# Where GpSimd issues the accumulating transfers of the first product's weight sums: behind the first mixer and about the norm, instead of inside the mixer

## The reference

```
# first block
h = rms_norm(x, ln_pre_mix);  proj = h @ w_in          # pooled features, q, k, v of 12 heads
mix = concat(multi_scale_pool(...), dilated_attention(rope(q), rope(k), v)) @ w_out
x = x + rms_norm(mix, ln_post_mix)
h = rms_norm(x, ln_pre_ffn)
f = (silu(h @ w_gate) * (h @ w_up)) @ w_down           # inner width 2816
x = x + rms_norm(f, ln_post_ffn)
# second block: three kinds of attention, then h + conv_gated_mlp(...) with w_up_2 and w_down_2,
# then a gated per-layer embedding with w_ple_gate_2 and w_ple_proj_2
```

## Time and profile before

| what | before |
| --- | --- |
| median of 3 runs | 1268.55 us (1266.91 to 1269.29) |
| profiled execution, its time | 1270.42 us |
| profiled execution, its span | 1268.7 us |
| TensorE busy | 1254.4 us, 99% of the span |
| GpSimd busy | 512.3 us, 40% |
| VectorE busy, ScalarE busy | 949.8 us, 729.0 us |
| mean granted clock of TensorE | 0.998 |

### The profile page before, as it was taken

The page is one execution under the profiler, slowest core; times in us unless marked ns, Lnnn a source line. Parts: engine busy times, 40 slices in busy tenths (PEclk is TensorE's granted clock), DMA queues, the critical chain, the costliest instruction groups (busy, mean ns, idle before and its releaser), DMA issues.

```text
span 1268.7 us, 22131 instructions
## 1 busy us (share of the span) xinstructions
PE 1254.4 (99%) x7684; PEld 1142.8 (90%) x7684; DVE 949.8 (75%) x1732; ACT 729.0 (57%) x1437; POOL 512.3 (40%) x578
## 2 busy tenths in 40 slices
PE   8999999999999999999999999999999999999998
PEld 7999978989999988889999999889889999887887
DVE  6687765799988878884566778457987777789754
ACT  5666744545555556656667778435455555556452
POOL 5576781256655500126788866310121313000000
PEclk9999999999999999999999999999999999999999
DMA  7699732335444467522377953232323333565221
GB/s 232 223 202 235 170 92 100 99 132 202 165 132 165 142 239 217 141 76 76 67 159 139 166 105 89 95 103 90 100 83 93 103 98 99 197 242 166 68 99 67
DMA packets 145607, 173.45 MB, mean 137 GB/s; under 512 B 25420, under 2 KB 111643, under 8 KB 145522
## 3 DMA queue, kind: packets, MB, share of 16 engines
q1 hardware_dynamic: 129600, 145.15, 35.8%
q0 software_dynamic: 15920, 27.18, 12.1%
q10 hardware_dynamic: 2, 0.00, 0.0%
HBM read 170.22 MB, written 39.85 MB: 166 GB/s over the span
## 4 chain that ended last, share of the span: by engine, by line
PE 88%; DVE 6%; POOL 2%; ACT 1%; DMA 1%; issue 1%; ACTq 0%; DVEq 0%; POOLq 0%
PE ps L2844 13%; PE ps L2845 13%; PE ps L2846 13%; PE ps L2963 6%; PE ps L2970 6%; PE ps L2965 6%; PE ps L3096 3%; PE ps L3100 3%; PE ps L3098 3%; PE ps L3140 3%; PE ps L3142 3%; PE ps L3141 3%; PE ps L3058 2%; DVE w_lo L2393 2%; PE ps L3046 1%; PE ps L3047 1%
## 5 line engine op out<-in xcount | busy, mean ns | idle before, releaser
L2844 PE MATMUL ps<-h_hi,w_hi 128*128 128x256 f32 (+1 forms) x748 | 238.3, 319 | 0.0
L2845 PE MATMUL ps<-h_lo,w_hi 128*128 128x256 f32 (+1 forms) x748 | 237.4, 317 | 0.0
L2846 PE MATMUL ps<-h_hi,w_lo 128*128 128x256 f32 (+1 forms) x748 | 237.2, 317 | 0.0
L2963 PE MATMUL ps<-w_hi,h_hi 128*128 128x384 f32 (+2 forms) x512 | 162.6, 328 | 0.0
L2965 PE MATMUL ps<-w_hi,h_lo 128*128 128x384 f32 (+2 forms) x512 | 157.9, 319 | 0.0
L2846 PEld LDWEIGHTS ps<-h_hi,w_lo 128*128 128x128 f32 x748 | 142.6, 191 | 9.6
L2844 PEld LDWEIGHTS ps<-h_hi,w_hi 128*128 128x128 f32 x748 | 142.6, 191 | 9.1 <-DVE h_lo L2140 0.3
L2845 PEld LDWEIGHTS ps<-h_lo,w_hi 128*128 128x128 f32 x748 | 142.7, 191 | 8.5
L1281 POOL TENSOR_TENSOR w_lo<-w_raw,w_hi 128x384 fp32r<-128x384 f32 (+2 forms) x114 | 120.5, 1131 | 26.9 <-ACT w_hi L1524 26.7
L2970 PE MATMUL ps<-w_lo,h_hi 128*128 128x384 f32 (+2 forms) x512 | 101.5, 319 | 0.0
L3140 PE MATMUL ps<-w_hi,st_hi 128*128 128x512 f32 x252 | 98.6, 391 | 0.5 <-DVE st_lo L2404 0.2
(11 more groups left out here) (327 smaller groups left out, 3338.9 us busy)
## 6 DMA issues: line engine op xcount, KB each, us to landing
w_raw<-in_w_up_dram SPq DMA_DIRECT2D x25, 1024.0 KB, 5.3
w_raw<-in_w_in_dram SPq DMA_DIRECT2D x69, 256.0 KB, 4.1
w_raw<-in_w_gate_dram SPq DMA_DIRECT2D x11, 1024.0 KB, 5.3
down_sums<-in_w_down_dram SPq DMA_DIRECT2D x18, 512.0 KB, 5.9
down_sums<-in_w_down_dram SPq DMA_DIRECT2D x36, 256.0 KB, 6.0
down_sums<-in_w_down_dram POOLq DMA_DIRECT2D x12, 768.0 KB, 8.3
down_sums<-down_sums POOLq DMA_DIRECT2D x12, 768.0 KB, 8.7
w_raw<-in_w_out_dram SPq DMA_DIRECT2D x8, 1024.0 KB, 5.1
```

What stands on the lines that cost most here:

```text
L2844: pe.matmul(out_, s_hi, m_hi, start=first and n == 0, stop=False, skip_group_check=True)
L2845: pe.matmul(out_, s_hi, m_lo, start=False, stop=False, skip_group_check=True)
L2846: mm = pe.matmul(out_, s_lo, m_hi, start=False, stop=last and n == len(pairs) - 1, skip_group_check=True)
L2963: pe.matmul(bank, h_hi[:, kb0 + i, tok], hi[:, i, :], start=half == 0 and i == 0, stop=False, skip_group_check=True)
```

## The change

The counts for the first mixer are gone, so its steps issue no accumulating transfer. `ADD_AFTER` keeps the counts for the second mixer, which doesn't change. A new helper issues one sum for all three groups. Behind the first mixer GpSimd issues T1 and T3 of the three groups (six transfers), then waits for `shared_filled` and fetches the gains as before, then issues the three T2, runs norm 1, issues the three T4, and goes on with the sums of blocks. Transfers, bytes and waits in `sums_added` are the same twelve.

```
-ADD_AFTER = ((9, 12, 15, 18, 20, 23, 25, 27, 29, 32, 35, 38), (8, 11, 14, 17, 20, 23, 26, 29, 32, 35, 38, 41))
+ADD_AFTER = (8, 11, 14, 17, 20, 23, 26, 29, 32, 35, 38, 41)
...
                         normed_units += 1
-                        if normed_units in ADD_AFTER[mx.b]:
-                            sums_added(mx.b, *ADD_ORDER[ADD_AFTER[mx.b].index(normed_units)])
+                        if mx.b == 1 and normed_units in ADD_AFTER:
+                            sums_added(1, *ADD_ORDER[ADD_AFTER.index(normed_units)])
...
+            def sums_of_groups(d, *names):
+
+                for name in names:
+                    for g in range(GROUPS):
+                        sums_added(d, g, name)
+
...
             mixer(mixers[0])
+            sums_of_groups(0, "T1", "T3")
             pool.wait_ge(shared_filled, n1.n["shared"])
             gain(1, gain_post[:, :], "ln_post_mix")
             gain(2, gain_pre[:, :], "ln_pre_ffn")
+            sums_of_groups(0, "T2")
             norm(1, True)
+            sums_of_groups(0, "T4")
             block_sums(0, 0, first=True)
```

## The result

The changed kernel takes 1283.75 us (median of 4 runs, 1283.15 to 1284.27), the kernel before 1268.92 beside it (median of 4, 1266.91 to 1269.99): a ratio of 1.0124 with a 95% interval of 1.011 to 1.0138 (the two medians divided give 1.0117). Forecast were 1284.3 us and slower. The profiled execution took 1283.44 us with a span of 1281.7, 13.0 more than the span of before.

What follows compares the result with a forecast made beforehand. TensorE, busy 1254.4 of 1268.7 us, was taken as the bound. Late gains, +14.7 us with the mixer's 4.1 us already spent, plus 1.0 for the clock gave +15.7 on the 1268.55 median: 1284.3 us, range 1273 to 1292.

Steps and rivals of the forecast that it cites:

- The line: Behind the first mixer, the gains queue in order behind six accumulates of 5.0 us each in GpSimd's DMA queue.
- G: Time at which gain_post lands: 225.0 us forecast, bounds 218.5 and 230.9, where it is wanted at 205.1.
- The chain behind it: In norm 1, 12.1 us from first y_scaled to second h_tok, putting tile 1's transposes at 237.1, +14.7 us.
- The clock: A low TensorE clock after some 16 us idle before the first transposes: +1 us, bounds 0 and 1.7.
- The mixer: In the first mixer, TensorE's stop falls from 2.9 to 0.4 us and all 1.7 us of clock return: -4.1 us.
- T2's waits: Behind the mixer, waiting for T1 landings holds GpSimd from norm 1 until 207 to 210, under the gains' delay: 0.
- T4's waits: Behind norm 1, the T2 land near 243, before norm 1 ends at 249.5, so nothing waits: 0.
- the block: At the block's first w_gate load, only the last T4 overlaps, by 3 us: taken as 0, bounds 0 and 2.
- A: Main case: late gains delay norm 1 and the mixer gets shorter; 1284.3 us, own range 1276.5 to 1291, chance 0.73.
- C: Accumulates run much faster in a row than alone: from no change down to 1264.9 us, chance 0.09.
- D: The gains overtake the accumulates, but T2's waits hold norm 1: 1267.5 us, 1264 to 1269, chance 0.07.
- E: Nothing collides behind the mixer: 1264.4 us, chance 0.02.

Runs made afterwards that it cites:

- gains_first: The changed kernel, but both gains are issued ahead of the six T1 and T3 transfers; 1273.4 us, ratio to before 1.0047.
- last_t4_ahead_of_gains: The kernel before, with only the third group's T4 moved behind the first mixer, ahead of the gains; 1266.17 us, ratio 0.9986.
- three_ahead: The changed kernel, but only the three T1 stand ahead of the gains, the T3 going behind norm 1 with the T4; 1270.58 us, ratio 1.0027.
- gains_by_sync: The changed kernel, but SyncE issues the two gains in its own queue, after waiting for shared_filled; 1272.81 us, ratio 1.0043.

## Why the prediction held, step by step

- **The line.** Right in kind and place. gain_post took 30.2 us (25 to 31 forecast), TensorE's stop on `h_tok` was 13.9 us (8 to 20 forecast), and with the gains first or in another queue the wait fell to 4.0 and 2.9 us. In size it was forecast a little too long: G = 225.0, measured 191.89 + 30.2 = 222.1. From 187 to 222 us GpSimd's queue used 85.3% of 16 engines and SyncE's 16.0%, 29.9 and 5.6 us of 35. Less the gains' 2.9, the six accumulates took 27.0 us, 4.5 each and not 5.0, and SyncE's loads 5.6 and not 7.2: one of them landed at 201.60 + 28.7 = 230.3, behind the gains. The forecast's 5.0 also had other traffic in it: from 678 to 684 GpSimd's queue alone used 80.0% of the engines, 4.8 us.
- **The chain behind it.** 12.1 us from the first y_scaled to the end of the second h_tok forecast, 234.21 - 222.14 = 12.1 measured. To set this end against TensorE's transposes (222.38) was off: before, these had 1.1 us in hand behind h_tok (221.30), while the h_lo behind it, done at 225.98, left none to the product at 226.03. The true term is VectorE's whole shift, 12.9 us.
- **The clock.** 1 us was added, next to nothing was paid: the work done at 0.50 stands ahead of tile 1's transposes and ends about as their h_tok does (234.38 and 234.21), and TensorE waits 0.77 us for h_lo after that. By chance this 1 us stood for the 1.1 us of the point above.
- **The mixer.** The step "I take the whole" was the one made on a single lot. The mechanism is right: T4 at 157.49, and nothing of the other eleven. The forecast's 4.1 us hold against that one profile (4.4 and 3.9 in the two kernels that move this T4 alone); against the median it is 0.8 to 1.5 us. (Its terms, 2.5 and 1.7, add up to 4.2.) The reciprocal that was said not to move was done at 161.37 and not at 162.05, and the late `prob` at 166.92 and not at 168.25, so the stop is gone altogether where 0.4 us were forecast. A stop of 1.8 us left the clock at 1.00, so the 1.7 us of clock belong to the worst of three profiles alone.
- **T2's waits, T4's waits, the block.** GpSimd was free at 205.9, forecast 207 to 210, under the gains' delay as said. The T4s waited for nothing, and TensorE's first product on block sums was late by the same 12.9 us (272.81 to 285.70): 0, as forecast. What the forecast had not seen is that the loads of w_gate and w_up have little slack once the gains' delay is gone.
- **The sum.** +15.7 us against spans that differ by 13.0, and against medians that differ by 14.8. The forecast carried over that the first profile lay 1.5 to 1.9 above its median; the one of the changed kernel lay 0.3 below its own. So part of the agreement of 1284.3 with 1283.75 is luck: 2.7 us too much in the sum, against 1.8 too little by the two profiles' places and 0.4 by a median of before that was 1268.55 then and 1268.92 beside the result.
- **The cases.** A came. C (a fast queue), D and E are excluded by the landings. D's mechanism is real, and is what `gains_first` shows, but at 6 us over an ordinary execution of before and not at 0, as the T1s there start 4.9 us later.

The only version that beat both kernels with an interval clear of 1 is `last_t4_ahead_of_gains`: 1266.17 us, 0.14% below before, a gain under the 0.2% named ahead.

## What to carry to other kernels

A small transfer that someone waits for must not be issued behind large ones in the same queue: ask for each DMA what is ahead of it in its queue at that moment, in us of engine time, not how large it is itself. Work that is off the path where it is, such as eleven of twelve transfers here, wins nothing by being moved; look for the single one whose wait reaches the bounding engine. And where the expected gain hangs on how soon a transfer lands, profile the kernel more than once before you trust its size.

## What was not expected of the hardware

- A load of 1024 KB that lands after 5.2 us alone took 18 to 29 us beside a line of accumulates in the other queue (19.9 and 28.7 in the changed kernel, 18.4 in `three_ahead`), while two gains of 512 KB took 7.9 and 10.3 (4.1 and 4.7 before).
- Issued in a row, the T3 transfers read 2.7 to 3.7 us each in the profile, alone some 1.3 us; GpSimd still issued one every 0.8 us.
- The DMA share stood at 1.09 to 1.13 for 35 us (197 to 232). In 214 to 222, as the last accumulates left the line and the gains moved, the same share moved 300 GB/s, against 231 in 203 to 214.
- TensorE's granted clock stayed at 1.00 behind idles of 1.2 and 1.8 us in the mixer, and fell behind one of 2.9 (0.62 in the 3 us behind it) and one of 13.9 (0.50). It fell behind one of 2.1 us too, in norm 1 of `gains_by_sync` (0.50 from 222 to 225).
